# The first gate third moved beside the large projection, and a rotary embedding moved into the output block

## The reference, cut to what matters

```python
shift, scale, gate = jnp.split(s_lat @ w_mod[layer] + b_mod[layer], 3, axis=-1)
shift_c, scale_c, gate_c = jnp.split(s_ctx @ w_mod[layer] + b_mod[layer], 3, axis=-1)
x_in = x * (1.0 + scale[:, None, :]) + shift[:, None, :]
c_in = h_ctx * (1.0 + scale_c) + shift_c
# layer 0: p = x_in @ w_in, pc = c_in @ w_in; latent attention; y = (mix * silu(gate part of p)) @ w_out
x = _post_norm(x, gate[:, None, :] * y, ln_g[layer], ln_b[layer])
...
# layer 1, the grouped attention: 16 query heads and 4 key heads of 128
k = _rms(kvp[..., :o_k - o_q].reshape(bsz, m, GQA_KV_HEADS, GQA_HEAD_DIM), k_norm)
q = _rms(qp.reshape(bsz, m, GQA_HEADS, GQA_HEAD_DIM), q_norm)
if rpos is not None:      # latent rows only
    k, q = _rope_2d(k, *rpos), _rope_2d(q, *rpos)
```

## Time and profile before

| What | us |
|---|---|
| median of 3 runs | 4289.64 (4287.26 to 4293.28) |
| the profiled execution: its own time | 4295.89 |
| its span in the trace | 4294.1 |
| PE busy | 3893.7 (91% of the span) |
| DVE busy | 1502.5 (35%) |
| ACT busy | 647.5 (15%) |
| POOL busy | 553.9 (13%) |
| granted TensorE clock, mean | 0.963 of full |

### The profile page before, as it was taken

The page is one execution under the profiler, slowest core; times in us unless marked ns, Lnnn a source line. Parts: engine busy times, 40 slices in busy tenths (PEclk is TensorE's granted clock), DMA queues, the critical chain, the costliest instruction groups (busy, mean ns, idle before and its releaser), DMA issues. The chain is left out here.

```text
span 4294.1 us, 59484 instructions
## 1 busy us (share of the span) xinstructions
PE 3893.7 (91%) x25244; PEld 1976.4 (46%) x25244; DVE 1502.5 (35%) x2698; ACT 647.5 (15%) x1330; POOL 553.9 (13%) x802
## 2 busy tenths in 40 slices
PE   8799997898949999887999999898988989989998
PEld 1245443344524444353444444453436667665443
DVE  0079996383211210432200013344533333332321
ACT  0000000102230110032110000143431122111000
POOL 0011110111100000110000012342103222231100
PEclk9899998999979999998999999998999999999999
DMA  8778875873265555625555578637763343333562
GB/s 294 258 263 324 294 276 195 288 264 107 86 254 199 169 183 169 217 73 206 179 167 168 166 251 304 204 121 237 257 224 93 92 122 98 92 102 139 201 224 104
DMA packets 357979, 822.59 MB, mean 192 GB/s; under 512 B 25468, under 2 KB 61652, under 8 KB 350796
## 3 DMA queue, kind: packets, MB, share of 16 engines
q1 hardware_dynamic: 257040, 485.08, 34.3%
q0 software_dynamic: 72544, 275.55, 17.8%
q10 hardware_dynamic: 28136, 58.22, 3.5%
HBM read 698.00 MB, written 120.77 MB: 191 GB/s over the span
## 5 line engine op out<-in xcount | busy, mean ns | idle before, releaser
L1029 PE MATMUL gemm_a_g_ps<-store_w,turned 128*128 128x512 f32 (+1 forms) x1152 | 455.5, 558 | 1.9 <-PEq L203 1.9
L812 DVE SCALAR_TENSOR_TENSOR pmods_acc<-pmods_w,cond,pmods_acc 128x512 f32<-128x512 f32 x570 | 402.8, 748 | 22.8 <-issue 0.9
L1029 PE MATMUL out_c_g_ps<-store_w,turned 128*128 128x512 f32 (+1 forms) x1024 | 399.3, 552 | 0.0
L1029 PEld LDWEIGHTS gemm_a_g_ps<-store_w,turned 128*128 128x128 f32 x1152 | 209.4, 191 | 247.5 <-issue 247.5
L2246 PE MATMUL scan_g_ps<-store_w,turned 64*64 64x512 f32 x2048 | 297.1, 623 | 19.1 <-PEq L1382 14.0
L1029 PEld LDWEIGHTS out_c_g_ps<-store_w,turned 128*128 128x128 f32 x1024 | 184.5, 190 | 213.8 <-issue 213.8
L1029 PE MATMUL att_a_g_ps<-store_w,turned 128*128 128x512 f32 x512 | 240.4, 603 | 12.8 <-PEq L3035 8.9
L1029 PE MATMUL gemm_hq_g_ps<-store_w,turned 128*128 128x512 f32 x512 | 222.3, 597 | 7.2 <-PEq L3035 7.2
L1029 PE MATMUL out_a_g_ps<-store_w,turned 128*128 128x512 f32 x512 | 221.8, 595 | 1.1 <-PEq L203 1.1
L1029 PE MATMUL out_a_g_ps<-store_w,turned_c 128*128 128x512 f32 x512 | 220.2, 592 | 0.0
L1029 PE MATMUL feat_g_ps<-store_w,turned 128*128 128x512 f32 x384 | 182.1, 623 | 21.5 <-ACT feat_stage L1629 13.6
(11 more groups left out here) (434 smaller groups left out, 4960.3 us busy)
## 6 DMA issues: line engine op xcount, KB each, us to landing
store_w<-in_w_in SPq DMA_DIRECT2D x160, 1024.0 KB, 5.5
pmods_w<-in_w_mod POOLq DMA_DIRECT2D x38, 2048.0 KB, 10.5
mods_w<-in_w_mod SPq DMA_DIRECT2D x48, 1024.0 KB, 9.3
store_w<-in_a_w_in SPq DMA_DIRECT2D x48, 1024.0 KB, 7.9
store_w<-in_c_w_in SPq DMA_DIRECT2D x48, 1024.0 KB, 5.1
store_w<-in_a_w_out SPq DMA_DIRECT2D x32, 1024.0 KB, 5.1
s_feat<-feat_o POOLq DMA_DIRECT2D x16, 1536.0 KB, 8.9
store_w<-in_w_branch SPq DMA_DIRECT2D x48, 512.0 KB, 3.6
```

The source lines that it names most:

```text
L812: v.scalar_tensor_tensor(a, src, x, a, ALU.mult, ALU.add)
L1029: mm = pe.matmul(out, act_tile(q * kq + k, tb), self.store.slot[i % self.store.NS][:, k, :width], start=(q == 0 and k == 0), stop=(q == 3 ...
```

## The change

The `mods` block multiplies only the first 4096 columns (8 chunks). The 4 gate chunks become the first jobs of gemm_a's weight store, with one "tile" each; their 16 multiplications go in turn to three row groups of one bank, ACT copies the three parts, and three DMAs store them. `sum_mods` adds the three parts (two more jobs). `MODS_EARLY` goes from 19 to 20. The four x tiles get four buffers of their own, and SP issues their loads, and behind them the store's first six, at the end of the `mods` block. The rotary embedding of the grouped attention leaves att_c's start and ends out_a, in the `z` buffers, with each 20-head item cut into a Q item of 16 heads and a K item of 4; its loads wait for the stores of the first 12 (latent) or 14 (context) tiles. att_c's lead goes from 86 to 10.

```diff
@@ gemm
             walk(sp, piece)
+            if then:
+                then(sp)
@@ rotate_heads
-        buf = [st.enter_context(nc.sbuf_tensor(f"{name}_x{s}", [P, big], F32)) for s in range(2)]
+        if buffers:
+            buf, tmp = buffers[0:2], buffers[2]
...
+            if wait_source:
+                wait_source(pool, n)
             pool.dma_start(buf[n % 2][:, :H * d].rearrange("p (h d) -> p h d", h=H), arr).then_inc(loaded[n % 2], 16)
@@ Ring.units
+                    lhs = act_tile(q * kq + k, tb)
+                    if len(tbs) == 1:
+                        to, first, last = self.thirds(out)[(q * kq + k) % 3], q * kq + k < 3, q * kq + k >= KT - 3
+                    else:
+                        to, first, last = out, q == 0 and k == 0, q == 3 and k == kq - 1
+                    mm = pe.matmul(to, lhs, self.store.slot[i % self.store.NS][:, k, :width], start=first, stop=last)
...
+    def thirds(self, out):
+        return [out[32 * r:32 * r + 2, :] for r in range(3)]
@@ out_norm_project
+        rope_programs = rope(st, z, wait_copies) if rope else None
...
+            if rope:
+                rope_programs[0](v)
...
+            if rope:
+                for tb in turns:
+                    after(pool, "dve", "turn", tb)
+                    after(pool, "act", "turn", tb)
+                rope_programs[1](pool)
@@ build
+        gate_jobs = [(I["w_mod"][0][:, 2 * D + a:2 * D + a + NCH], ("gate",), None, lambda r, a=a: gate_parts[:, r, a:a + NCH])
+                     for a in range(0, D, NCH)]
+        jobs = gate_jobs + a_first + lat_jobs + a_gate
...
+        def load_x_and_weights(sp):
+            x_early.load(sp)
+            store.load_first(sp)
+             [(I["w_mod"][0][:, 0:2 * D], (0,), None, lambda tb: mods[0])], kmap="pk", then=load_x_and_weights)
-        MODS_EARLY = 19
+        MODS_EARLY = 20
-        project(nc, "gemm_a", store, xt(512), a_first, mods_beside)
+        project(nc, "gemm_a", store, lambda k, tb: cond[:, 0, k, :] if tb == "gate" else xt(512)(k, tb), gate_jobs + a_first, mods_beside)
+                 + [(gate_parts[c], mods[0, c:c + 1, 2 * D:]) for c in range(2)])
+        def rope_c(st, z, wait_copies):
+            gains = ((C_Q, 16, 0), (C_K, 4, 1))
+            items = [(rows(proj_c, tb)[:, a:a + 128 * h].rearrange("t (h c) -> t h c", h=h), h, 128, tb, [(0, h, gi)])
+                     for tb in LAT for a, h, gi in gains]
+            items += [(rows(proj_c, tb)[:, C_K:C_V].rearrange("t (h c) -> t h c", h=4), 4, 128, None, [(0, 4, 1)]) for tb in (2, 3)]
+                                lambda eng, n: wait_copies(eng, 12 if n < 4 else 14))(st)
-        attend_and_project(nc, "att_c", store, ident, GroupedPlan(proj_c, mix_c, tiled), 128 ** -0.5, 128, xc, c_gate, 86, rope)
+        attend_and_project(nc, "att_c", store, ident, GroupedPlan(proj_c, mix_c, tiled), 128 ** -0.5, 128, xc, c_gate, 10)
```

More of the change, by code:

```diff
@@ L80, in load_first, with gemm @@
             sp.dma_start(self.wbuf[0][:, ks, :], self.src[:, ks, 0:NCH]).then_inc(self.w_loaded[0][q], 16)
-def gemm(nc, name, act_tile, KT, segments, kmap="kp", side=None, early=None):
+def gemm(nc, name, act_tile, KT, segments, kmap="kp", side=None, early=None, then=None):
     NQ = 4
@@ L188, in _, with turn @@
                 wait(act, stored[s], 16 * tiles[s])
-def turn(nc, name, ident, tiles, width, out, norm=False, scale=None, shift=None, weights=None):
+def turn(nc, name, ident, tiles, width, out, norm=False, scale=None, shift=None, early=None):
     KT = width // P
@@ L203, in turn @@
     with ExitStack() as st:
-        buf = [st.enter_context(nc.sbuf_tensor(f"{name}_a{s}", [P, width], F32)) for s in range(2)]
+        slots = len(tiles) if early else 2
+        buf = early.buf if early else [st.enter_context(nc.sbuf_tensor(f"{name}_a{s}", [P, width], F32)) for s in range(2)]
         fac = [st.enter_context(nc.sbuf_tensor(f"{name}_b{s}", [P, 2 * terms_max - 1, width], F32))
@@ L209, in turn @@
         ps = [st.enter_context(nc.psum_tensor(f"{name}_ps{s}", [P, NCH], F32)) for s in range(4)]
-        loaded = [nc.alloc_semaphore(f"{name}_loaded{s}") for s in range(2)]
+        loaded = early.loaded if early else [nc.alloc_semaphore(f"{name}_loaded{s}") for s in range(2)]
         read_out = [nc.alloc_semaphore(f"{name}_read_out{s}") for s in range(2)]
@@ L299, in _, with __init__, load @@
                     mm.then_inc(turned, 1)
+class EarlyTiles:
+    def __init__(self, nc, st, name, sources, width):
+        self.sources = sources
+        self.buf = [st.enter_context(nc.sbuf_tensor(f"{name}_x{n}", [P, width], F32)) for n in range(len(sources))]
+        self.loaded = [nc.alloc_semaphore(f"{name}_x_loaded{n}") for n in range(len(sources))]
+    def load(self, sp):
+        for n, src in enumerate(self.sources):
+            sp.dma_start(self.buf[n][:, :], src).then_inc(self.loaded[n], 16)
 def columns(nc, name, ident, jobs):
@@ L415, in _, with rotate_heads @@
                 act.wait_ge(stored[s], 16 * ((len(tiles) + 1 - s) // 2))
-def rotate_heads(nc, name, items, cos_sin, gains=None):
+def rotate_heads(nc, name, items, cos_sin, gains=None, buffers=None, wait_source=None):
     big = max(i[1] * i[2] for i in items)
@@ L820, in sum_mods @@
 def sum_mods(nc, name, jobs):
-    NC = 3 * D // NCH
+    counts = [src.shape[1] // NCH for src, dst in jobs]
+    upto = [sum(counts[:n]) for n in range(len(jobs) + 1)]
     with ExitStack() as st:
@@ L852, in _ @@
                 pe.wait_ge(loaded[n % 2], 16 * (n // 2 + 1))
-                for c in range(NC):
-                    m = n * NC + c
+                for c in range(counts[n]):
+                    m = upto[n] + c
                     if m >= 24:
                         pe.wait_ge(copied, m - 23)
-                    pe.matmul(place(m), ones[:, :], part[n % 2][:, c * NCH:(c + 1) * NCH],
+                    pe.matmul(place(m), ones[:jobs[n][0].shape[0], :], part[n % 2][:jobs[n][0].shape[0], c * NCH:(c + 1) * NCH],
                               start=True, stop=True).then_inc(summed, 1)
@@ L865, in _ @@
                     act.wait_ge(stored[n % 2], 16 * (n // 2))
-                for c in range(NC):
-                    m = n * NC + c
+                for c in range(counts[n]):
+                    m = upto[n] + c
                     act.wait_ge(summed, m + 1)
                     act.activation(row[n % 2][:, c * NCH:(c + 1) * NCH], place(m), ACT.Copy).then_inc(copied, 1)
-                act.wait_ge(copied, NC * (n + 1))
-                act.dma_start(dst, row[n % 2][:, :]).then_inc(stored[n % 2], 16)
+                act.wait_ge(copied, upto[n + 1])
+                act.dma_start(dst, row[n % 2][:, :src.shape[1]]).then_inc(stored[n % 2], 16)
             for s in range(2):
@@ L974, in load @@
             n, q = i // 4, i % 4
-            src = self.jobs[n][0].rearrange("(k p) n -> p k n", p=P)
+            src = self.jobs[n][0].rearrange("(k p) n -> p k n" if self.jobs[n][1] != 1 else "(p k) n -> p k n", p=P)
             kq = src.shape[1] // 4
@@ L1058, in project @@
         stage = [st.enter_context(nc.sbuf_tensor(f"{name}_stage{n}", [P, NCH], F32)) for n in range(4)]
-        copied = nc.alloc_semaphore(f"{name}_copied")
+        n_thirds = sum(len(tbs) == 1 for w, tbs, func, dst in projections)
+        thirds = [[st.enter_context(nc.sbuf_tensor(f"{name}_third{n}{r}", [2, NCH], F32)) for r in range(3)]
+                  for n in range(n_thirds)]
+        copied, third_stored = nc.alloc_semaphore(f"{name}_copied"), nc.alloc_semaphore(f"{name}_third_stored")
         tile_stored = [nc.alloc_semaphore(f"{name}_tile_stored{n}") for n in range(4)]
@@ L1084, in _ @@
                 g.wait_tile(act, t)
+                if len(tbs) == 1:
+                    for r, piece in enumerate(g.thirds(g.out(t))):
+                        last = act.activation(thirds[t % 4][r][:, :], piece, ACT.Copy)
+                    last.then_inc(copied, 1)
+                    act.wait_ge(copied, t + 1)
+                    for r in range(3):
+                        act.dma_start(dst(r), thirds[t % 4][r][:, :]).then_inc(third_stored, 16)
+                    act.sem_inc(tile_stored[t % 4], 16)
+                    continue
                 act.activation(stage[t % 4][:, :w.shape[1]], g.out(t), func).then_inc(copied, 1)
@@ L1130, in out_norm_project, with wait_copies @@
         stored = [nc.alloc_semaphore(f"{name}_stored{n}") for n in range(4)]
+        def wait_copies(eng, count):
+            for s in range(4):
+                eng.wait_ge(stored[s], 16 * ((count + 3 - s) // 4))
+        rope_programs = rope(st, z, wait_copies) if rope else None
         block = st.enter_context(nc.Block())
@@ L3162, in build @@
         columns(nc, "cols", ident,
-                [([vrows(mods[l, 0]), vrows(mods[l, 1])], [vrows(biases[l])] * 2, cols[l][:, :]) for l in range(1)]
```

(12 more changed lines are left out.)

47 lines of the change are left out of this document (24 added, 23 removed).

## The result

The changed kernel takes 4303.03 us (median of 20 runs, 4293.25 to 4320.15) and the kernel before 4289.33 in the runs beside it (20 runs, 4282.68 to 4302.63): a ratio of 1.0034, 95% interval 1.0025 to 1.0042. It is slower, by 13.7 us in the medians. The forecast was 4299.3, +9.7. The profiled execution took 4299.90 us (span 4298.1), 4.0 more than the one before (span 4294.1).

The account below looks back on a forecast made before the run. PE, busy 91% of the span, was taken as the main bound, with each block closed by its last engine. Terms 14.5 - 16.3 + 5.4 + 33.7 - 27.6 = +9.7 us on 4289.64 gave 4299.3, 8-in-10 range 4272 to 4318.

Parts of the forecast that it names:

- Modulations and head: First modulations four chunks shorter, -54.7 us; columns' DVE start at about 196, then projection block start at 217.4.
- the prediction's frame: Clock of the trace before the change; the shortened modulations' 54.7 us are subtracted only at the end.
- B: Start of the projection block, where the gate chunks now come first; forecast at 217.4 on the earlier trace's clock.
- Gate stretch: Gate chunks ahead of the projection: SP gets a third of the bytes, so projection passes start 86 us after block start.
- The rival of equal bytes (65 us): Gate chunks: SP's loads keep up better, projection starts after 65 us, total -11, 4278 us; better supply had chance 0.17.
- the one of PE as the bound: Gate chunks: packed passes pace the stretch, PE needs 19 us, total -46, 4243 us; chance 0.02.
- hidden by 50 us: Projection block: DVE's 20 side chunks end at 703, before PE's end at 758.9, so they do not close it.
- Latent attention's start, its wait, the sums: Latent attention starts 14.5 us later, its PE wait and slow passes go (-16.3), modulations' sums grow by 5.4.
- Rotary embedding in out_a: End of out_a: the moved rotary items delay PE's next start to 1762.4, +33.7 us, bounds 24 and 42.
- The shorter tail (24): End of out_a: rotary tail costs 24 us instead of 33.7, total 0, 4290 us; chance 0.16.
- forecast -27.6: att_c: waits for first loads and DVE's scaling go, ACT table loads add 1; -27.6 us, bounds -20 and -29.

Follow-up runs that it names:

- experiment 3: Changed kernel, but POOL issues its first side-modulation load only when the projection's first quarter has landed; 4294.09 us, ratio 1.0002 to the kernel before.
- experiment 6: Changed kernel with all 16 multiplications of a gate chunk in one row group of the bank; 4301.26 us, one run.
- Experiment 7: Changed kernel with att_c's lead at 86 again instead of 10; 4321.17 us, ratio 1.0082 to the kernel before.
- rotary alone: Kernel before with only the rotary embedding moved to the end of out_a, all 12 chunks kept in the modulations; 4303.48 us, ratio 1.0016 to the kernel before.

## Why the prediction was right

**Modulations and head.** Eight copies, the last at 127.33 instead of 183.03: -55.7 against -54.7. The columns' DVE instruction comes at 141.19 + 54.7 = 195.9 in the prediction's frame, where 196 was forecast; that agrees with small loads that wait behind the ten quarters, though no run takes it apart. B came at 159.9, forecast 217.4 - 54.7 = 162.7. The missing 2.8 are the turn's: its first tile came 0.8 sooner, three pitches took 12.1 instead of 13.0 (the last tiles' 16 passes 1.97 us instead of 3.68), and the first gate pass followed by 4.3 us, not 5.5.

**Gate stretch.** The deciding term: 86.7 us against 86. It came from one row of two microseconds in the trace before (equal packets, unequal bytes), and experiment 3 shows that POOL's traffic is the cause: without it the stretch is 35.4. That the number came out within 1 us is partly luck. The step gave SP 11.1 MB by B + 86 where it needed 11.5, which at 0.13 MB/us is 3 us more; measured from 160 to 246.6, SP moved 12.45 MB and POOL 20.15, not 21.5, and part of SP's was for later quarters. PE waited 45.5 us in it, not some 60, since its passes ran at half the clock (last section). The Trainium skill ("DMA: Bandwidth & Descriptors", Queues, rings and completion order) says that an engine takes turns between its queues a whole packet at a time; by that rule, the equal counts agree. The rival of equal bytes (65 us) is refuted by the 1.01 against 2.05 MB, and the one of PE as the bound by experiment 6. DVE's side chunks ended with POOL's store at 645.7, 55 us before PE's last copy; "hidden by 50 us" was a slip for 56.

**Latent attention's start, its wait, the sums.** +10.6 against +14.5: 2.8 from the head, 1.0 less of PE in the projection, 0.9 less from the last copy to the next block, and 0.7 back in the stretch. The wait of 14.7 in the earlier trace rows is 0.35 now, and the stage takes 16.2 less, forecast 16.3 (no run changes the number of side chunks alone). The sums are 5.0 longer, forecast 5.4. So to mix_a the change is -0.6 us where +3.6 was forecast.

**Rotary embedding in out_a.** From mix_a to att_c's first pass +35.7, forecast +33.7, the largest miss behind the projection block: DVE started 9.7 us after POOL's first load (forecast 8), the Q items took 20.4 and 21.6 (20.3), the K item behind the first 12.0 (11.7). From the second K item's start at 1735.04 to PE's next pass at 1763.77 it took 28.7, forecast 28.3. The shorter tail (24) is refuted.

**att_c.** 209.1 us instead of 236.6: -27.5, forecast -27.6. Experiment 7 shows that 15.3 of it hang on the lead, as the step said. PE's waits for ACT are 4.5, of which the forecast priced 1, and the small turn waits, 1.6 in all, didn't fall by 0.8. Against that stands PE's busy time, which fell by 3.8 us and not by the 1.9 of the step. These misses cancel, so the agreement within 0.1 us is luck; that the two large waits go is not. The block's stretch (columns as in the last section), first of the kernel before, then after:

```profile
1728.60:1965.20 236.60, 199.82 (x752) 107.32 (x752) 98.43 (x178) 58.13 (x113) 42.64 (x61) 0.95 0.40 135
```

```profile
1763.70:1972.80 209.10, 195.99 (x752) 104.39 (x752) 51.12 (x140) 64.04 (x118) 26.27 (x44) 0.98 0.37 121
```

The passes are the same 752; the granted clock is 0.98 instead of 0.95.

**What is not settled.** The trace's terms give 7.6 us at mix_c, the spans 4.0, the medians 13.7. The part behind mix_c is the same code in all ten kernels, and its length in their single traces goes from 2325.3 (after) to 2332.5 (rotary alone), with 2328.9 before. So a single trace cannot carry 5 us; the sum was within that of the result, and I can't say which term the medians' other 6 us belong to. The sizes of both halves, near zero and +8 to +9, are shown; that the whole is 0.34% and not 0.18% is not explained. One thing on record moves with the time: among 29 runs of the kernel before, the mean granted clock goes from 0.965 in the shortest (4279.49) to 0.958 in the longest (4309.93), and among the 20 after from 0.957 (4293.25) to 0.953 (4320.15). Whether it is the cause, no run shows.

## What to carry to other kernels

Work moved off a PE-bound stage into the next block pays only where its loads find cover: with the four gate chunks at the head of the block the gate half was worth nothing, with them between projection chunks 54.5 us in the traces (47 by the ratios). Before loads are moved to a place where another engine's queue is full, look at packets and bytes of each queue in a few microseconds where both are full; the share per queue, not the total, sets how long the moved work waits. Where one engine waits for a store, loads the next and also computes a small step of the item between, look whether the step can go ahead of the wait; the traces show what it waits for, but no run here moved it.

## What the runs showed of the hardware

With both full, these two DMA queues shared by packets, not by bytes: 514 packets of 4 KB against 510 of 2 KB, 0.26 against 0.13 MB/us, while SP's queue alone moved 3.09 MB in 8 us (0.39).

Narrow passes in three row groups overlap: 32 of them, each 2 columns of weights by 512, take 5.3 us (0.166 each), in one group 0.43 each, both at a granted clock of 1.00. The Trainium skill ("TensorEngine Tiling (Array Packing)", Theoretical Speedup) allows up to 4 times at a width of at most 32; three groups gave 2.6 here, and no run used four.

The same eight packed passes took 3.57 us where PE had idled 4.5 us or more before, and 1.88 where it had idled 1. The stretches (us, busy time of PE, PEld, DVE, ACT and POOL, granted clock, DMA share, GB/s) of the changed kernel show the clock beside it:

```profile
175.00:178.70 3.70, 3.57 (x8) 0.35 (x8) 3.55 (x6) 0.00 (x0) 0.00 (x0) 0.50 1.03 383
237.40:239.40 2.00, 1.88 (x8) 0.27 (x8) 1.93 (x4) 0.00 (x0) 0.00 (x0) 1.00 1.04 385
```

The granted clock was 0.50 (1.2 GHz) in the one and 1.00 (2.4 GHz) in the other. It cost nothing here, since the loads came later still, up to the last: the first projection quarter was issued at 220.53 and landed 25.7 us later, at 246.2, 0.4 before its first pass.

```profile
store_w<-in_a_w_in SPq DMA_DIRECT2D x1, 1024.0 KB, 25.7
```
